# A transformer block on one core: the first feed-forward stage starts with four quarters of input rows in four accumulator banks, with the modulation units computed one by one between them

## The reference, cut to what matters

```python
def rmsnorm(x, g): return x * rsqrt(mean(x * x) + eps) * g
def modulate(n, shift, scale): return n * (1 + scale) + shift
def swiglu(n, w_gate, w_up, w_down): return (silu(n @ w_gate) * (n @ w_up)) @ w_down

mod = silu(c) @ w_ada + b_ada                  # c: 1024, w_ada: 1024 x 9216
sh1, sc1, gt1, sh2, sc2, gt2, sh3, sc3, gt3 = split(mod, 9)
n = modulate(rmsnorm(h, g_ffn1), sh1, sc1)     # h = x: 256 tokens x 1024
h = h + 0.5 * gt1 * swiglu(n, w1_gate, w1_up, w1_down)     # hidden width 2816
n = modulate(rmsnorm(h, g_mix), sh2, sc2)
h = h + gt2 * hybrid_mixer(n, w_in, w_pool, pool_scale, w_out)
n = modulate(rmsnorm(h, g_ffn2), sh3, sc3)
h = h + 0.5 * gt3 * swiglu(n, w2_gate, w2_up, w2_down)
...
# then two attention layers (window, block-sparse) and a last rmsnorm
```

## Time and profile before

| | us |
|---|---|
| three runs | 739.37, 743.51, 752.68 |
| median | 743.51 |
| span of the profiled execution, from its first to its last instruction | 737.9 |
| TensorE busy in the span | 707.5 (96%) |
| VectorE, ScalarE busy | 487.3 (66%), 368.3 (50%) |
| mean granted TensorE clock | 0.977 of full |

### The profile page before, as it was taken

The page is one execution under the profiler, slowest core; times in us unless marked ns, Lnnn a source line. Parts: engine busy times, 40 slices in busy tenths (PEclk is TensorE's granted clock), DMA queues, the critical chain, the costliest instruction groups (busy, mean ns, idle before and its releaser), DMA issues.

```text
span 737.9 us, 14334 instructions
## 1 busy us (share of the span) xinstructions
PE 707.5 (96%) x6000; PEld 663.3 (90%) x6000; DVE 487.3 (66%) x740; ACT 368.3 (50%) x567; POOL 67.0 (9%) x65
## 2 busy tenths in 40 slices
PE   6599999999999999989999999999999999999996
PEld 4299999999998988869999999998988889988896
DVE  3469788877865446566545445457789976788843
ACT  4154434344354346647343343446666676666643
POOL 0000064000000690000000000001300001000000
PEclk9589999999998999999999999999999999999999
DMA  9998999999956763174656565563433333553301
GB/s 343 382 362 301 337 361 329 350 329 325 337 198 215 262 208 115 59 234 161 207 180 214 178 209 186 177 214 120 148 124 123 119 119 115 172 172 115 115 2 57
DMA packets 104293, 152.60 MB, mean 207 GB/s; under 512 B 2616, under 2 KB 88380, under 8 KB 104124
## 3 DMA queue, kind: packets, MB, share of 16 engines
q1 hardware_dynamic: 103876, 151.48, 59.7%
q10 hardware_dynamic: 376, 0.55, 0.2%
HBM read 150.97 MB, written 1.05 MB: 206 GB/s over the span
## 4 chain that ended last, share of the span: by engine, by line
PE 44%; DVE 7%; ACT 3%; issue 1%; ACTq 0%; DVEq 0%
PE acc L1394 6%; PE acc L1396 6%; PE acc L1395 6%; PE sc L1394 5%; PE sc L1395 5%; PE sc L1396 5%; DVE wlo L929 2%; PE acc L1699 1%; PE acc L1700 1%; PE acc L1701 1%; ACT whi L603 1%; PE stat L1405 1%; PE sc L1588 1%; DVE vp L1115 1%; ACT vp L730 1%
## 5 line engine op out<-in xcount | busy, mean ns | idle before, releaser
L929 DVE TENSOR_TENSOR wlo<-raw,whi 128x2048 fp32r<-128x2048 f32 x104 | 240.9, 2319 | 115.5 <-ACT whi L603 115.3
L603 ACT ACTIVATE whi<-raw 128x2048 fp32r<-128x2048 f32 x105 | 200.2, 1909 | 67.4 <-PE sc L1396 57.6
L1394 PE MATMUL sc<-nhi,whi 128*128 128x256 f32 x704 | 195.9, 278 | 2.0 <-DVE nlo L1354 1.6
L1395 PE MATMUL sc<-nlo,whi 128*128 128x256 f32 x704 | 195.5, 278 | 0.0
L1396 PE MATMUL sc<-nhi,wlo 128*128 128x256 f32 x704 | 195.4, 278 | 0.0
L1394 PEld LDWEIGHTS sc<-nhi,whi 128*128 128x128 f32 x704 | 133.4, 189 | 2.5 <-issue 2.5
L1395 PEld LDWEIGHTS sc<-nlo,whi 128*128 128x128 f32 x704 | 133.4, 190 | 0.0
L1396 PEld LDWEIGHTS sc<-nhi,wlo 128*128 128x128 f32 x704 | 133.3, 189 | 0.0
L1394 PE MATMUL acc<-nhi,whi 128*128 128x256 f32 x376 | 109.4, 291 | 0.8 <-DVE nlo L986 0.6
L1395 PE MATMUL acc<-nlo,whi 128*128 128x256 f32 x376 | 104.4, 278 | 0.0
L1396 PE MATMUL acc<-nhi,wlo 128*128 128x256 f32 x376 | 104.3, 277 | 0.0
(11 more groups left out here) (248 smaller groups left out, 1105.7 us busy)
## 6 DMA issues: line engine op xcount, KB each, us to landing
ada<-in_w_ada_dram SPq DMA_DIRECT2D x23, 1024.0 KB, 7.5
raw<-in_w_gate_dram SPq DMA_DIRECT2D x22, 1024.0 KB, 5.5
raw<-in_w_up_dram SPq DMA_DIRECT2D x22, 1024.0 KB, 6.0
raw<-in_w_down_dram SPq DMA_DIRECT2D x22, 1024.0 KB, 4.9
raw<-in_w_out_dram SPq DMA_DIRECT2D x12, 1024.0 KB, 4.9
raw<-in_w_in_b_dram SPq DMA_DIRECT2D x10, 1024.0 KB, 5.2
xo<-in_w_ada_dram SPq DMA_DIRECT2D x9, 1024.0 KB, 7.4
raw<-in_w_in_a_dram SPq DMA_DIRECT2D x9, 1024.0 KB, 5.3
```

Of the source, the lines that this page charges most:

```text
L603: nc.scalar.activation(whi[:, u % NS], raw[:, u % NS], ACT.Copy).then_inc(hi_done, 1)
L929: nc.vector.tensor_tensor(wlo[:, u % NS], raw[:, u % NS], whi[:, u % NS].bitcast(F32), ALU.subtract).then_inc(lo_done, 1)
L1394: mm(to, stat_hi, mov_hi, start=first, stop=False, skip_group_check=True)
L1395: mm(to, stat_hi, mov_lo, start=False, stop=False, skip_group_check=True)
```

## The change

The start is written anew on all engines.

- **Loads.** The first two blocks of gate and up columns (512 columns of each) come not as four units of 256 columns but as four quarters of the input rows: quarter g holds row chunks 2g and 2g+1 of 512 gate and 512 up columns, in two transfers of 0.5 MB (`load_quarter`). The first eight units of `w_ada` come one by one, each 8 row chunks by 256 columns, in the order scale 0, shift 0, scale 1, shift 1 and so on (`START_UNITS`), into three places (`start_at`). Quarter g is issued ahead of the scale and shift units of its chunks.
- **Modulation.** `start_rows(n)` sums one whole unit in four column groups, `start_copy`, `start_sums` (two matmuls with one column of ones) and `start_out` follow for each unit: eight rounds in place of two.
- **TensorE.** `first_quarter(g)` multiplies the two chunks of quarter g for four banks (`sc[0]`, `sc[1]`, `tp0`, `stat`), 12 matmuls a bank, 48 a quarter. Gate and up of blocks 0 and 1 are complete only when quarter 3 is. The rows of the next scale unit stand between the third and the fourth bank of a quarter.
- **VectorE and ScalarE.** `vp`, `nhi` and `nlo` are made two chunks at a time; the first unit's `high` and `low` come earlier; entry of `ffn(0)` is rewritten: two hidden blocks read from four banks, and eight `chain` instructions of units 8 to 11 stand among the `low`s.

Matmul counts of the large products are the same: 4 times 48 before and after.

```diff
-START_QUADS = (4, 0)
+START_UNITS = (4, 0, 5, 1, 6, 2, 7, 3)
...
+            def load_quarter(g):
+                if g >= NS:
+                    sp.wait_ge(lo_done, g - NS + 1)
+                for n in range(2):
+                    sp.dma_start(rows2(raw, g % NS)[:, :, 2 * n * UC:2 * (n + 1) * UC],
+                                 ffn_w[0][n][:, 2 * g:2 * g + 2, 0:2 * UC]).then_inc(landed[g % NS], 16)
...
             for n in range(8):
-                if n == 4:
-                    load_unit(0, ffn_w[0][0][:, :, 0:UC])
-                if n >= 4:
-                    sp.wait_ge(row_done, n - 3)
-                k, col = n % 4, START_QUADS[n // 4] * UC
-                sp.dma_start(start_slots[n % 4], w_ada_v[:, 2 * k:2 * k + 2, col:col + 4 * UC]).then_inc(ada0_in[n % 4], 16)
-            sp.wait_ge(row_done, 5)
-            load_unit(1, ffn_w[0][1][:, :, 0:UC])
+                if n % 2 == 0:
+                    load_quarter(n // 2)
+                if n == 2:
+                    sp.wait_ge(x_t, DC)
+                elif n > 2:
+                    sp.wait_ge(row_done, n - 2)
+                col = START_UNITS[n] * UC
+                sp.dma_start(start_at[n % 3], w_ada_v[:, :, col:col + UC]).then_inc(ada0_in[n % 3], 16)
...
-                    sp.wait_ge(row_done, 6)
-                    load_unit(2, gate[:, :, UC:2 * UC])
-                    load_unit(3, up[:, :, UC:2 * UC])
+                    load_unit(4, down[:, 0:2, :])
+                    load_unit(5, gate[:, :, 2 * UC:3 * UC])
                     sp.wait_ge(row_done, MOD_START)
                     load_ada(8)
+                    load_unit(6, up[:, :, 2 * UC:3 * UC])
                     load_ada(9)
-                    load_unit(4, down[:, 0:2, :])
-                    for j in range(1, FB - 1):
+                    load_unit(7, down[:, 2:4, :])
+                    load_ada(10)
+                    load_ada(11)
+                    for j in range(2, FB - 1):
...
-            high(0)
-            norm_high(0)
-            high(1)
-            high(2)
+            for g in range(4):
+                norm_high(0, range(2 * g, 2 * g + 2))
+                if g == 2:
+                    act.wait_ge(ffn_used, 1)
+                if g < 3:
+                    high(g + 1)
...
+            low(0)
             inverse_deviation(0)
...
+            for g in range(4):
+                start_copy(2 * g)
+                start_out(2 * g)
+                dve.wait_ge(mod_done, 2 * g + 1)
+                link(coefficient(0, 2 * g, 2 * g + 2))
+                for m in range(2 * g, 2 * g + 2):
+                    nc.vector.scalar_tensor_tensor(out=vp[:, m], in0=hT[:, m], scalar=norm_gain(0, m), in1=rstd[:, :],
+                                                   op0=ALU.mult, op1=ALU.mult).then_inc(t_done, 1)
+                start_copy(2 * g + 1)
+                start_out(2 * g + 1)
+                dve.wait_ge(mod_done, 2 * g + 2)
+                for m in range(2 * g, 2 * g + 2):
+                    dve.wait_ge(nhi_done, m + 1)
+                    nc.vector.scalar_tensor_tensor(out=nlo[:, m], in0=vp[:, m], scalar=norm_shift(0, m),
+                                                   in1=nhi[:, m].bitcast(F32), op0=ALU.add,
+                                                   op1=ALU.subtract).then_inc(nlo_done, 1)
+                if g < 3:
+                    low(g + 1)
...
+            def first_quarter(g):
+                pe.wait_ge(lo_done, g + 1)
+                hi, lo = rows2(whi, g % NS), rows2(wlo, g % NS)
+                for n, bank in enumerate(first_banks):
+                    col = (n % 2) * 2 * UC + (n // 2) * UC
+                    for i in range(2):
+                        ch = 2 * g + i
+                        if n == 0:
+                            pe.wait_ge(nlo_done, ch + 1)
+                        for m in range(2):
+                            at = slice(col + m * P, col + (m + 1) * P)
+                            ins = split_product(bank[:, m * S:(m + 1) * S], hi[:, i, at], lo[:, i, at], nhi[:, ch],
+                                                nlo[:, ch], ch == 0 and m == 0, ch == DC - 1)
+                    if g == 3 and n < 3:
+                        ins.then_inc(first_done, 1)
+                    if g < 3 and n == 2:
+                        start_rows(2 * g + 2)
+                ins.then_inc(ffn_used, 1)
+                if g < 3:
+                    start_sums(2 * g + 2)
...
-                    gate(base, 0, norm=k)
-                    up(base + 1, 0)
+                    for g in range(4):
+                        if g == 0:
+                            start_rows(0)
+                            start_sums(0)
+                        start_rows(2 * g + 1)
+                        start_sums(2 * g + 1)
+                        first_quarter(g)
```

169 lines of the change are left out of this document (94 added, 75 removed).

## The result

The changed kernel takes 753.68 us (median of four runs, 749.66 to 753.82) against 743.05 us for the kernel before on the same chip (four runs, 739.37 to 752.68): ratio 1.0133, with a 95% interval of 1.0094 to 1.0173. Medians and ranges in this document are of all executions, while a ratio with its interval leaves out those over 1.5% above the fastest of their kernel (up to three of six in the later comparisons), so it differs somewhat from the quotient of the two medians beside it. The changed kernel's profiled execution has a span of 751.7 us and an own time of 753.62, so that 1.9 us lie around the span, not the 5.6 that the forecast took from the median of before. Between the two profiled spans, 737.9 and 751.7, lie 13.8 us.

A forecast was written before the change was run, and what follows sets the result against it. The start was taken as bound by arrivals, then by chains between quarters: 23.1 + 24.75 + 13.8 + 3.2 + 0.5, plus 0.2 and 2.8, is 68.4 against 61.2. Span 745.0 plus 5.6 gave 750.5 us, range 740 to 759.

The forecast's parts named there:

- What bounds the start: Start before the change: bound by arrivals, as eight units of `w_ada` must land before TensorE's large work.
- The first quarter: Start: after two units and a 4.6 us chain the first large matmul comes at 23.1 us, 13.3 us earlier.
- What is added between quarters: Between quarters: the modulation chain recurs three times, 13.8 us, plus 3.2 us for scale-unit rows inside quarters 0 to 2.
- T: End of the start: the time at which 192 large matmuls are done, 61.2 us before, forecast at 68.4.
- The clock: TensorE's clock in the gaps between quarters: lost in two of three at 1.4 us each, 2.8 us.
- The entry of the loop: First down unit: waits 0.5 us for hidden block 0; VectorE's queue fits ahead of unit 8 by 0.3 us.
- (c): Rival at the loop's entry: VectorE or the loads are late, giving 752 to 758 us; chance 0.12.
- The sum at T: End of the fourth quarter: all terms of the start summed to 68.4 against 61.2 us, 7.1 us later.
- (a): Rival for the start: chain between quarters hidden, arrivals alone bind, 11.6 us earlier, 731.9 us; chance 0.15 with half-way forms.
- arrivals hide: Loads in the start: the last unit lands at 36 to 41 us, while quarter 3 needs it near 56.
- (b): Rival for the start: clock stays low throughout, 17.5 us a round, 25 us later, 768.5 us; chance 0.08.
- (d): Rival: a mere shift, first gap's price and gain cancel, +4.3 us or less, 745 to 748; inside the forecast's 0.65.

The follow-up runs named there:

- inside: Changed kernel with the next quarter's whole modulation chain laid between the banks of the present quarter, only large matmuls between quarters: 742.15 us, ratio 1.0041 to the kernel before.
- entry: Changed kernel with VectorE's `low` of unit 4 halved around the first hidden product, so TensorE needn't wait at loop entry: 748.9 us, ratio 1.0165 to the kernel before.
- pause: Changed kernel with TensorE waiting for ScalarE's `high` of unit 5 ahead of the first down unit: 749.4 us, ratio 1.0082 to the kernel before.
- pause_again: Second run of the changed kernel with the added TensorE wait ahead of the first down unit: 747.79 us, ratio 1.0124 to the kernel before.
- again: Changed kernel run once more without an edit: 749.03 us, ratio 1.004 to the kernel before.
- touch: Kernel before with one added one-column matmul into an unused bank ahead of the first down unit: 745.57 us, ratio 1.0032 to the kernel before.
- before_pause: Kernel before with TensorE waiting until ScalarE has rounded unit 6, ahead of the first down unit: 747.37 us, ratio 1.0025 to the kernel before.

## Why the prediction came out

**What bounds the start.** Right. The chance of 0.65 went to the case in which the chain between quarters takes back what the earlier start gives, and that is what the profile shows.

**The first quarter.** Forecast 23.1, measured 22.84. The chain of 4.6 us from the sums to the first large matmul took 4.46 there (18.38 to 22.84).

**What is added between quarters.** Right in kind, a little too large: 3 x 4.34 = 13.0 us for 13.8 (`mod` stands 0.5 and 2.8 us behind the first sums, for 0.7 and 3.1). The rows of the second unit lie inside the chain, as said. The rows of the scale unit inside a quarter cost 1.2 us of stream each (from 40.50 to 41.93 in quarter 1, less two matmuls), 3.6 for 3.2. The forecast also said that TensorE idles some 2.5 us of each gap. `inside`, which takes away only the place of the small matmuls, measures this: a round shrinks from 13.60 to 11.57 (quarter 0) and from 11.12 to 9.25 (quarter 1), by 2.03 and 1.87 us; quarter 2's shrinks by 3.52, of which 1.64 is the clock's fall. The sum is the 7.42 at T.

**The clock.** The term that was mis-sized at T. Forecast: 2.8 us, two of three gaps at 1.4. Measured: one fall, in quarter 2, which took 8.42 us (47.56 to 55.98) where quarter 1 took 6.78 (36.44 to 43.22): 1.64 us. The two later profiles of the same program have it at the same place. But `entry`, `pause` and `pause_again`, whose TensorE order is the same up to the end of the quarters, lost it twice, at quarters 1 and 3, and in `pause` the last large matmul of quarter 3 begins at 68.50, where the forecast had T at 68.4. One fall or two is thus open to an execution. The Trainium skill, "TensorE: Matmul & The Clock Gate", section "HAM oscillation — how this bites in real kernels", says of its example, short bursts parted by waits for loads, that each burst begins throttled. The gaps here hold small matmuls and no idle stretch over 1.6 us. The traces agree for one or two of three gaps of the same length and disagree for the others; the sum by that rule, 5 us more at T, was not seen.

**The entry of the loop.** Forecast 0.5 us, measured 0.23 of waiting. VectorE's queue fitted: TensorE had no wait in the loop (idle 0.0 in the groups). The ScalarE side of rival (c) did happen without effect. Timeline of the changed kernel, ScalarE:

```profile
81.99 1.92 ACT L622 ACTIVATE whi<-raw 128x2048 fp32r<-128x2048 f32 x1 [3.47 <-DMA raw<-in_w_gate_dram]
87.57 1.92 ACT L622 ACTIVATE whi<-raw 128x2048 fp32r<-128x2048 f32 x1 [3.66 <-DMA raw<-in_w_up_dram]
```

Two landings were 3.5 us late for ScalarE and still early enough for TensorE.

**The sum at T.** Forecast 68.4, measured 66.25, and against before +5.4 instead of +7.1 us (the forecast's own terms give 68.35 - 61.16 = 7.2). The clock has 1.2 of the 2.1 us between them, the gaps 0.8.

**The step that failed** is the one behind T: "In the loop VectorE has the same work as before and gains on TensorE, so what is lost or won at T stays till the end", with "behind it the same rhythm of 16.3 us a block". TensorE had no waits, as said, but the rhythm was 158.37 / 152.32 of the old one, 16.96 us a block: 6.05 us in the first loop, more than the change did at T. The runs show that a slow first loop isn't fixed to the change: `again` has the fast loop with the same instructions, and then lies 742.3 - 737.9 = 4.4 us above before, of the 5.3 that its T gives. `touch` and `before_pause` show the kernel before with the slow pace. But the change makes it more likely, by the estimate above: 0.41 more slow loops an execution, at some 6 us each, are about 2.5 of the 11.0 us that lie between the mean spans (750.8 and 739.9). With equal numbers of slow loops after lies 7.4 us above before (mean 743.4 against 736.0, none slow) or 8.3 (751.7 against 743.4, one slow), of which T explains 5.4. The first two profiles have the like of the rest, 2.4 us, in the clock between the loops; over all executions this isn't shown. What sets the pace stays open.

**The way to 750.5.** The span was forecast at 745.0 and measured at 751.7; the forecast time adds 5.6 us where 1.9 lie around a span. The other 3.7 are the distance of the median execution of before from the profiled one, which had no slow loop. So the 753.68 is near 750.5 partly by luck: an allowance for which the forecast had no cause stood where the slow loop came. With a span of 742.3, as in `again`, and 1.9 about it, the changed kernel takes 744.2; with that of the first profile, whose first loop is slow, 753.6.

**Rivals.** (a), arrivals alone, did not happen: the steps between quarters were there. That arrivals hide is borne out twice, by the empty queue at 52 and 55 us and by `inside`, which starts its last quarter at 52.90 without a wait for a landing. (b), a low clock throughout, did not happen: the clock was back about 5 us into quarter 0 and 3.4 us after its fall in quarter 2. (c), a late VectorE or late loads, came without its price, as told above. (d), +4.3 us for a mere shift, is near the 5.4 measured at T.

## What to carry to other kernels

Small dependent steps between pieces of a large product cost their whole latency each time they recur, however early the first piece starts; laid between the banks of the piece ahead (here 7.4 us at T for the same instructions), they cost only their own TensorE time. Before a difference of one per cent between two profiles is explained, compare the distance from one large matmul to the next far away from the change, and profile the unchanged program a second time; a program with two paces is compared over many executions, or over those with the same number of slow loops. A gain at one place is worth what the path behind it keeps: compare milestones (first large matmul, end of the stage, end of the loop) before totals.

## What the runs showed of the hardware

TensorE's large split matmuls (256 columns, full clock 1.00, no waits) ran at one of two paces, 113.3 or 117.8 ns from start to start, in the same program: 152.3 or 158.4 us for the first loop, 153.4 or 159.4 for the second. Of 28 loops in 14 profiles, 16 were fast and 12 slow, and none lay between. The pace was different in the two loops of one execution in 6 of 14, changed at breaks in the middle of an execution in both directions (at T from 113.6 to 117.8 in the changed kernel, from 117.8 to 113.3 in `again`), and was kept as long as no break came, in `before` from 42.0 us through T to the end of the first loop. The Trainium skill, "TensorE: Matmul & The Clock Gate", section "Wait — 56ns, not 53.3ns?", gives one distance for back-to-back matmuls at full clock, N/2.4 + 2.5 ns; for 256 columns that makes an estimate of 109.2, and the runs measured 113.3 and 117.8 instead. What sets the pace is not found: a small matmul, a removed wait and an added pause at the loop's entry each left it undecided in a single execution. Over 144 executions the estimate has half of those of `before` without a slow loop, 61% with a pause of more than 1 us ahead of the loop, and 18% with a short break there.

The clock's fall at a gap wasn't fixed either. Three gaps with the same small matmuls lost it once in the three profiles of the changed kernel, each time at quarter 2, and twice in those of `entry`, `pause` and `pause_again`, at quarters 1 and 3; the one in the changed kernel cost 1.64 us. In `inside`, where no gap is left, it didn't fall again before the end of the first loop.
